# Attention outputs feature by row on two column halves of the array, from probabilities scaled before they are turned

## The reference

```python
# first block: 16 heads of 64, 2 key/value heads, the 64 best keys of an indexer
p = jax.nn.softmax(logits, axis=-1).astype(dt)
o = jnp.einsum('bqgrk,bqkgd->bqgrd', p, v_sel)
...
return out @ w_o
```

## Time and profile before

| | us |
|---|---|
| median of 3 runs | 965.53 |
| lowest, highest | 965.35, 970.52 |
| the profiled execution | 965.12 |
| its span, first to last instruction | 963.1 |

### The profile page before, as it was taken

How to read it: one execution, slowest core, us unless ns; L and a number is a source line. 1 busy time by engine, 2 the same in 40 slices (tenths; PEclk the granted TensorE clock), 3 DMA queues, 4 the chain that set the end, 5 groups by cost and what they waited for, 6 DMA issues and landing times.

```text
span 963.1 us, 12213 instructions
## 1 busy us (share of the span) xinstructions
PE 940.8 (98%) x4867; PEld 785.8 (82%) x4867; DVE 594.3 (62%) x958; ACT 458.0 (48%) x609; POOL 151.4 (16%) x127
## 2 busy tenths in 40 slices
PE   8989999999999999999999999999999999999996
PEld 6868788888888999987888888878788788888885
DVE  5874773645558578877755546484223467677775
ACT  5774353524434441443534334354656456555653
POOL 3292300000006300011000000040355201001010
PEclk9999999999999999999999999999999999999999
DMA  9981475665547552225766556459433455565541
GB/s 301 195 157 50 169 220 175 193 199 175 181 169 238 194 184 88 88 90 173 241 188 201 179 182 208 143 171 323 132 132 88 153 176 176 196 193 178 175 131 44
DMA packets 104376, 164.88 MB, mean 171 GB/s; under 512 B 4011, under 2 KB 74714, under 8 KB 104320
## 3 DMA queue, kind: packets, MB, share of 16 engines
q1 hardware_dynamic: 101056, 152.61, 48.4%
q0 software_dynamic: 3264, 11.49, 5.7%
HBM read 159.89 MB, written 4.19 MB: 170 GB/s over the span
## 4 chain that ended last, share of the span: by engine, by line
PE 91%; ACT 3%; DVE 3%; issue 1%; DMA 1%; POOL 1%; DVEq 0%; POOLq 0%; ACTq 0%
PE PG L1790 12%; PE PG L1792 12%; PE PG L1791 12%; PE PA L1790 12%; PE PA L1792 12%; PE PA L1791 11%; PE PA L2235 3%; PE PG L1926 1%; PE TB L2365 1%; PE TB L2038 1%; PE TB L1935 1%; PE TB L1781 1%; ACT whi L590 1%; PE TB L1943 1%; PE PA L2192 1%
## 5 line engine op out<-in xcount | busy, mean ns | idle before, releaser
L599 DVE TENSOR_TENSOR wlo<-raw,whi 128x2048 fp32r<-128x2048 f32 (+1 forms) x125 | 291.2, 2346 | 66.2 <-ACT whi L590 66.1
L590 ACT ACTIVATE whi<-raw 128x2048 fp32r<-128x2048 f32 (+1 forms) x142 | 268.4, 1907 | 54.4 <-PE PA L1792 22.2
L1790 PE MATMUL PG<-whi,xlo 128*128 128x512 f32 x548 | 217.6, 397 | 0.2 <-DVE xlo L1097 0.2
L1792 PE MATMUL PG<-whi,xhi 128*128 128x512 f32 x548 | 213.7, 390 | 0.0
L1791 PE MATMUL PG<-wlo,xhi 128*128 128x512 f32 x548 | 213.3, 389 | 0.0
L1792 PEld LDWEIGHTS PG<-whi,xhi 128*128 128x128 f32 x548 | 102.9, 188 | 22.0
L1790 PE MATMUL PA<-whi,xlo 128*128 128x512 f32 (+1 forms) x292 | 116.8, 400 | 3.8 <-DVE xlo L1097 3.5
L1790 PEld LDWEIGHTS PG<-whi,xlo 128*128 128x128 f32 x548 | 103.0, 188 | 20.8 <-DVE xlo L1097 0.6
L1791 PEld LDWEIGHTS PG<-wlo,xhi 128*128 128x128 f32 x548 | 103.1, 188 | 20.0
L1792 PE MATMUL PA<-whi,xhi 128*128 128x512 f32 (+1 forms) x292 | 112.5, 385 | 0.0
L1791 PE MATMUL PA<-wlo,xhi 128*128 128x512 f32 (+1 forms) x292 | 112.1, 384 | 0.0
(11 more groups left out here) (291 smaller groups left out, 1245.5 us busy)
## 6 DMA issues: line engine op xcount, KB each, us to landing
raw<-in_ffn_w_gate SPq DMA_DIRECT2D x44, 512.0 KB, 4.0
raw<-in_ffn_w_up SPq DMA_DIRECT2D x44, 512.0 KB, 5.0
raw<-in_ffn_w_down SPq DMA_DIRECT2D x22, 1024.0 KB, 4.9
raw<-in_w_up SPq DMA_DIRECT2D x44, 512.0 KB, 4.6
raw<-in_hgrn_w_in SPq DMA_DIRECT2D x16, 1024.0 KB, 5.3
raw<-in_w_qkv SPq DMA_DIRECT2D x12, 1024.0 KB, 5.2
raw<-in_w_down SPq DMA_DIRECT2D x11, 1024.0 KB, 4.9
raw<-in_att_w_o SPq DMA_DIRECT2D x4, 1024.0 KB, 5.5
```

The lines of the kernel that those rows point to most:

```text
L590: nc.scalar.activation(whi[:, g, 0:n_], raw[:, s, 0:n_], ACT.Copy).then_inc(S("w_hi"), 1)
L599: nc.vector.tensor_tensor(wlo[:, s, 0:n_], raw[:, s, 0:n_], whi[:, g, 0:n_].bitcast(F32), ALU.subtract).then_inc(S("w_lo"), 1)
L1790: mm(dst, xl[:, k, rows], whi[:, g, cols], start=first, stop=False)
L1792: return mm(dst, xh[:, k, rows], whi[:, g, cols], start=False, stop=last_)
```

## The change

Each head's `pr` is multiplied by its reciprocal row sum before it is turned (`normalize`, two instructions with the reciprocal as a per-partition pointer), so reciprocals are taken per head. `pv(p)` then makes both heads of a pair: the 64 value columns are the weights, 128 turned probabilities are streamed, and head c writes partitions 64c to 64c+63 of the output, products of the two heads alternating. It waits for the copies of both heads. The results come out with features on partitions. DVE copies them from PSUM to `oT` (`outputs`), so `orow`, `turn_out_rows` and their events fall away; `out_hi` and `out_lo` read `oT` in SBUF. The projection waits on `o_lo` in place of a bank.

```diff
-                pe.wait_ge(S("prob" + tag), 2 * hd + 2)
+                pe.wait_ge(S("normed" + tag), 2 * hd + 2)
...
-                pe.wait_ge(S(("odd_turned" if hd % 2 else "even_turned") + tag), hd // 2 + 1)
-                o = TB[:, e % 2, 384:512]
-                mm(o[:, 0:HD], pT[:, hd % 4, 0:P], value(hd, 0), start=True, stop=True)
-                mm(o[:, HD:P], pT[:, hd % 4, P:2 * P], value(hd, 0), start=True, stop=False)
-                mm(o[:, HD:P], pT[:, hd % 4, 2 * P:3 * P], value(hd, 1), start=False, stop=True)\
-                    .then_inc(S("pv" + tag), 1)
+                pe.wait_ge(S("even_turned" + tag), p + 1)
+                pe.wait_ge(S("odd_turned" + tag), p + 1)
+                def product(c, r, k):
+                    hd = 2 * p + c
+                    o = TB[HD * c:HD * c + HD, turned_p[tag][2 * p + r] % 2, 384:512]
+                    return mm(o, value(hd, k), pT[:, hd % 4, (r + k) * P:(r + k + 1) * P], start=k == 0, stop=k == r)
+                product(0, 1, 0)
+                product(1, 0, 0)
+                product(0, 1, 1)
+                product(1, 1, 0)
+                product(0, 0, 0)
+                product(1, 1, 1).then_inc(S("pv" + tag), 1)
```

On DVE:

```diff
+                def normalize(hd, ready):
+                    vec.wait_ge(S("vec_chain"), ready)
+                    for r, (a, b) in enumerate(((0, 128), (128, 384))):
+                        ve_.tensor_scalar(pr[:, hd % 4, a:b], pr[:, hd % 4, a:b], arec[:, hd, r:r + 1], None, ALU.mult)\
+                           .then_inc(S("normed" + tag), 1)
+                def outputs(p):
+                    vec.wait_ge(S("pv" + tag), p + 1)
+                    for r in range(RT):
+                        e = turned_p[tag][2 * p + r]
+                        ve_.tensor_copy(oT[:, p, r * P:(r + 1) * P], TB[:, e % 2, 384:512]).then_inc(bank_free(e), 1)
...
                 first_minima()
+                for hd in range(2):
+                    normalize(hd, reciprocals(hd))
                 minima(2)
                 minima(3)
                 for p in range(PAIRS):
+                    ahead, after = p + 2 < PAIRS, p + 1 < PAIRS
+                    if p in (3, 5, 7):
+                        out_lo(tag, p // 2 - 1)
                     turn_out(2 * p)
+                    if after:
+                        ready = reciprocals(2 * p + 2)
                     if ahead and p not in late:
                         minima(2 * p + 4)
+                    if after:
+                        normalize(2 * p + 2, ready)
+                    outputs(p)
+                    if after:
+                        ready = reciprocals(2 * p + 3)
                     if ahead and p not in late:
                         minima(2 * p + 5)
+                    if after:
+                        normalize(2 * p + 3, ready)
...
             def out_lo(tag, g):
-                lo_of_bank(flat(xlo[:, 2 * g:2 * g + 2, :]), turned_o[tag][g], flat(xhi[:, 2 * g:2 * g + 2, :]))
+                nxhi[0] += 1
+                vec.wait_ge(S("x_hi"), nxhi[0])
+                tiles = slice(2 * g, 2 * g + 2)
+                ve_.tensor_tensor(flat(xlo[:, tiles, :]), flat(oT[:, tiles, :]), flat(xhi[:, tiles, :]).bitcast(F32),
+                                  ALU.subtract).then_inc(S("o_lo" + tag), 1)
```

More of the change, by code:

```diff
@@ L205, in build @@
         pT = carve(4, 384)
-        orow = carve(RT, D)
+        oT = carve(KT, T)
         amin = carve(HQ, 2)
@@ L289, in build @@
         squares = carve(2, HALF)
+        orow = oT.rearrange("p a b -> p (a b)").rearrange("p (r c) -> p r c", r=RT)
         rel_dram = nc.dram_tensor("rel_scratch", [HQ, P, REL_W], F32, kind="Internal").ap()
@@ L303, in build @@
         n = 0
-        turned_p, turned_o = {"": [], "2": []}, {"": [], "2": []}
+        turned_p = {"": [], "2": []}
         for name, k in (("x", 4), ("c0", 2), ("cq", 1), ("ki", 1), ("qi", 4), ("kk", 1), ("q", 4), ("heads", ""),
@@ L315, in build @@
                         n += 4
-                    if p in OUT_AFTER:
-                        turned_o[k].append(n)
-                        n += 1
                 continue
@@ L670, in out_hi @@
             def out_hi(tag, g):
-                e = turned_o[tag][g]
-                turned(e)
-                ac.activation(flat(xhi[:, 2 * g:2 * g + 2, :]), TB[:, e % 2, :], ACT.Copy).then_inc(S("x_hi"), 1)
+                for r in range(RT):
+                    freed(act, turned_p[tag][4 * g + 2 + r])
+                tiles = slice(2 * g, 2 * g + 2)
+                ac.activation(flat(xhi[:, tiles, :]), flat(oT[:, tiles, :]), ACT.Copy).then_inc(S("x_hi"), 1)
             def attention(tag, probs_made):
@@ L1118, in turn_out, with reciprocals @@
                     ve_.tensor_copy(pT[:, hd % 4, :], TB[:, e % 2, 0:384]).then_inc(S("even_turned" + tag), 1)
[L1120 to L1131, removed]
+                def reciprocals(hd):
+                    vec.wait_ge(S("prob" + tag), 2 * hd + 2)
+                    return link.mark(ve_.reciprocal(arec[:, hd, :], asum[:, hd, :]))
+                def normalize(hd, ready):
[5 more added lines that the diff above has]
+                    vec.wait_ge(S("pv" + tag), p + 1)
+                    for r in range(RT):
+                        e = turned_p[tag][2 * p + r]
+                        ve_.tensor_copy(oT[:, p, r * P:(r + 1) * P], TB[:, e % 2, 384:512]).then_inc(bank_free(e), 1)
                 minima(0)
@@ L1138, in attention @@
                 for p in range(PAIRS):
-                    if p and p - 1 in OUT_AFTER[:3]:
-                        out_lo(tag, OUT_AFTER.index(p - 1))
+                    ahead, after = p + 2 < PAIRS, p + 1 < PAIRS
+                    if p in (3, 5, 7):
+                        out_lo(tag, p // 2 - 1)
                     turn_out(2 * p)
-                    ready = reciprocals(p)
-                    ahead = p + 2 < PAIRS
+                    if after:
+                        ready = reciprocals(2 * p + 2)
                     if ahead and p not in late:
                         minima(2 * p + 4)
-                    vec.wait_ge(S("vec_chain"), ready)
-                    output(2 * p)
+                    if after:
[3 more added lines that the diff above has]
+                        ready = reciprocals(2 * p + 3)
                     if ahead and p not in late:
                         minima(2 * p + 5)
-                    output(2 * p + 1)
+                    if after:
+                        normalize(2 * p + 3, ready)
                     if p in late:
@@ L1889, in closing @@
                             last.then_inc(S("w_used"), 1)
[L1891 to L1901, removed]
             def out_tile(U, tag, j, q):
@@ L1906, in out_tile @@
                 if q == 0:
-                    parts_ready(turned_o[tag][j])
+                    pe.wait_ge(S("o_lo" + tag), j + 1)
                     pe.wait_ge(S("w_lo"), U + j + 1)
@@ L1937, in turn, with pv @@
                     last.then_inc(S("t_full"), 1)
[L1939 to L1946 removed]
+                def pv(p):
+                    pe.wait_ge(S("even_turned" + tag), p + 1)
[10 more added lines that the diff above has]
+                    product(1, 1, 1).then_inc(S("pv" + tag), 1)
                 logits(0)
@@ L1956, in attention @@
                         logits(p + 2)
-                    pv(2 * p)
-                    pv(2 * p + 1)
+                    pv(p)
                     outputs_made(p)
@@ L1961, in attention @@
                         logits(p + 2)
-                    if p in OUT_AFTER[:3]:
-                        turn_out_rows(tag, OUT_AFTER.index(p))
             def out_closing(U, tag):
-                closing((U + 2, 4, None, None, lambda r: parts_ready(turned_o[tag][2])),
-                        (U + 3, 6, None, None, lambda r: parts_ready(turned_o[tag][3])),
-                        between=lambda: turn_out_rows(tag, 3))
+                closing((U + 2, 4, None, None, lambda r: pe.wait_ge(S("o_lo" + tag), 3)),
+                        (U + 3, 6, None, None, lambda r: pe.wait_ge(S("o_lo" + tag), 4)))
             def down_row(u, k0, r, xh, xl, between=None):
```

## The result

The changed kernel takes 997.45 us (median of 4 runs, 995.32 to 999.75), the kernel before 966.16 beside it (965.35 to 970.52): ratio 1.0328, 95% interval 1.0311 to 1.0346. It is slower by 31.3 us; I had forecast 993, 27.6 over, in a range of 967 to 1006. The profiled execution of the changed kernel took 997.4 us, its span is 32.5 us longer than that of the earlier trace rows.

What follows compares the result with a forecast made beforehand. TensorE, on the last-ending chain for 91% of the span, was taken as the bound. First block +16.6, third block +10.0 and clock +1 made +27.6 us on a 965.5 us median: 993 us, range 967 to 1006.

Steps and rivals of the forecast that it cites:

- The mechanism: Both attention blocks: multiplies and out_lo wait for a running GpSimd op, each multiply costing up to one such op.
- rival 1: Both blocks: neither multiplies nor out_lo collide with GpSimd; -4.2 us, 961.3 us, not slower; chance 0.10.
- rival 2: Both blocks: only out_lo collides with GpSimd; +3.2 us, 968.7 us; chance 0.08.
- Rival 3: DVE always gets in between two GpSimd ops, third block's pairs 2 and 3 escape; about 980 us; chance 0.10.
- The multiply's undisturbed price: DVE, per head: multiplies at two elements a step, about 0.29 and 0.36 us, 0.5 in sequence.
- Rival 4: New products: column halves not side by side, 1.45 us instead of 0.8; 1001 us with collisions, 970 without; chance 0.10.
- Which heads are caught: First block: heads 0 and 1 normalised 6.6 us late, head 4 6.7 more; first projection 14.8 us later.
- The clock: TensorE after its pauses: possible fall to 1.2 GHz, bounds 0 and about 2 us per pause; 1 us added.
- The closings: End of first and third blocks: out_lo(3) waits for a GpSimd op, TensorE stands; +3.3 us each.
- The third block: Third block: turn(0) 3.15 us late, collisions in pairs 2 and 3 and the closing; +10.0 us in sum.
- the pair 2 term: Third block: head 6's multiply meets two GpSimd ops, holding output copies; +2.6 us for pairs 0 to 2.
- Without collisions: Both blocks with no waits for GpSimd: first block -1.0, third block -3.2, together -4.2 us.

Runs made afterwards that it cites:

- e1: Changed kernel with each multiply by a reciprocal also asking for an accumulated output: 977.89 us, ratio 1.0133 to the kernel before.
- e2: Changed kernel with ACT's split of each attention's last weight unit moved behind out_hi(3), so GpSimd's last subtraction starts behind out_lo(3): 988.84 us, ratio 1.0240.
- e4: Changed kernel with GpSimd's subtractions of the two attentions cut into four pieces of 512 columns each: 977.36 us, ratio 1.0124.
- e10: First block as before; third changed, with accumulating multiplies, moved split, four-piece subtractions, and a pair's products by head instead of alternating: 964.35 us, ratio 1.0002.
- e3: Changed kernel with both accumulated output on the multiplies and each attention's last weight unit split after out_hi(3): 968.48 us, ratio 1.0035.
- e8: Changed kernel with accumulating multiplies, last weight unit split after out_hi(3), and the attentions' GpSimd subtractions in four pieces: 964.29 us, ratio 0.9991.

## Why the prediction was right, step by step

**The mechanism** was the predicted one: DVE instructions that go at double pace or read two tensors from SBUF stand still beside GpSimd's. e1 (form changed, wait gone), e2 (GpSimd moved, wait gone) and e4 (GpSimd shortened, wait shortened) each turn one knob of it; rival 1, that there is none, is out, and so is rival 2. Rival 3 had one half right, that DVE gets in between two GpSimd instructions, and not the other, that pairs 2 and 3 of the third block escape: head 7 was caught, and out_lo(0) behind it held TensorE for 2.12 us in pair 3. The multiply's undisturbed price, taken as 0.29 and 0.36 us, was 0.28 and 0.345.

**Rival 4** is out: column halves run side by side. The new products of one pair of the third block took 0.80 us up to the next one, against 1.36 in the earlier trace rows:
```profile
767.15 0.88 PE L1949 MATMUL TB<-work 128*64 128x128 f32 x12
767.95 0.50 PE L1804 MATMUL PA<-whi,xlo 128*128 128x512 f32 x1
```
The 0.8 was right to 0.01, and e10 shows that it hangs on the order of issue. One slip stands in its working: the logits' eight records stream 2 x 128 + 2 x 256 columns twice, without a further factor of 2; the 1.3 us given there is right for that.

**Which heads are caught** I had wrong in the first block. I had head 0 and 1 lose a GpSimd instruction each and head 4 two in a row. In the trace a head's second multiply got in before the next GpSimd instruction (head 0 was done at 59.9, beside a start at 59.6), and heads 1, 3 and 5 were caught, one instruction each: pauses of 4.17, 4.17 and 4.35. As I read it, each wait held back ACT's next weight split, so that the GpSimd instruction which waits for that split met the next pair at the same point: behind turn(1) ACT split weights at 67.29 and 76.49, and GpSimd started at 69.33 and 78.91. TensorE's first projection came 18.0 us later than before (91.46 against 73.42), where I had 14.8; of the 18.0 up to 6 are low clock.

**The clock** is the term that was mis-sized most. I added 1 in all, with bounds of 0 and 2 per pause. In the windows above TensorE was busy 10.6 us at 0.50 in the first block, 5.0 at 0.53 behind its closing and 5.0 at 0.50 behind turn(0) of the third. At 2.4 GHz that is 5.3, 2.4 and 2.5 us less. The windows at the ends of these stretches (0.83 from 60 to 65, 0.78 from 85 to 90, 0.79 from 115 to 120, 0.84 from 705 to 710) hold some 2 us more: about 12 in all, an upper estimate as not all of it set the end. Then waits and gains were worth at least 19 net, where I had 26.6: two errors of opposite sign. That the sum came within 4 us is thus partly luck; the mechanism is not. The range had room for 10 us of clock. The changed kernel's profiled execution also had a clock of 0.81 from 50 to 55 us, before any changed code had run, and logits(1) came 1.2 us later than before. It cost nothing: in e2 logits(1) was early, and from logits(0) to logits(2) both kernels take 13.1 us, since GpSimd's end set turn(1).

**The closings**: +3.3 each forecast. By e2 both together are 8.6, by e1 against e3 9.4; TensorE stood 3.13 us in the first block and 3.12 in the third, and in the first the clock came on top.

**The third block** was +10.0 forecast and 10.4 measured from its first logits to the end: TensorE stood 3.15 us before turn(0), the figure of the forecast, and then heads 7 and 9 and out_lo(0) between them were caught.
```profile
709.55 0.87 PE L1937 MATMUL TB<-ident,work 128*128 128x128 f32 x3 [3.15 <-DVE work L1131]
```
The agreement is luck in part. Up to logits(4) the loss was 5.2 us, where I had 5.75; of the 5.2 up to 2.9 are low clock behind turn(0), and the pair 2 term didn't come, as head 6's first multiply got in after 0.78 us. From logits(4) to (7) it was 2.7, where I had 1.0, and from there to the end 2.5, where I had 3.25.

**Without collisions** I had 4.2 us of gain. e8, with only short ones left, comes level. By the table (pairs and what follows them) block 3 gained 2.3 us of the forecast 3.2, and block 1 lost 3.1 instead of gaining 1.0; up to 1.6 of the 3.1 may be that one execution's. There the dearer multiplies add 0.4 us to a loop of 4.2 (4.56 apart in e1 and e3), out_lo(0) took 1.32 us beside a piece instead of 0.69, and the clock was 0.66 in two windows (65 to 70 and 75 to 80). How the loss divides between these was not tried apart.

## What to carry to other kernels

Before putting a vector instruction beside GpSimd work, look at what it reads and at what pace it goes: one that needs the shared port costs up to the whole length of GpSimd's instruction, whatever its own length. Three cheap ways out worked here: another form of the instruction, another order of the other engine's work, shorter instructions there. And count a pause of TensorE with the clock behind it; here three pauses of 12.7 us together had some 6 us of it behind them.

## What the runs showed of the hardware that I had not expected

- With GpSimd's instructions queued without a gap, a waiting multiply got in after the one that it had met, and ended 0.08 us behind it; one multiply of e4, which came 0.09 us before a piece's end, stood for the next piece too. The multiply right behind it got in with it at heads 0 and 6 of the changed kernel, but in e4 twice only, and seven times it stood for a whole further piece. GpSimd paid where both got in: a piece took 1.39 us instead of 1.27, a whole one 4.72 instead of 4.57.
- The same pause in the same place was followed by different clocks: behind 3.12 us in the third block's closing it was 1.00 in the changed kernel and 0.78 (765 to 770 us) in e1.
- fp32 products of two column halves start 6 or 7 ns apart when issued in turn, and a pair's six take 0.81 us; in head order 1.08.
- A full fp32 product of 128 columns takes 0.22 us at 2.4 GHz, twice a transposition's 0.11.
